# Prompt chunks of both mixers: two products from float32 to three float32r products of high and low parts

## What is computed

```python
# mLSTM, for each chunk of tokens (q, k: per head 128 wide; v: 256 wide)
A   = einsum('blhd,bshd->bhls', qc, kc) * exp(D - m_t)
num = einsum('bhls,bshv->bhlv', A, vc) + w_inter * einsum('blhd,bhdv->bhlv', qc, C)
den = sum(A) + w_inter * einsum('blhd,bhd->bhl', qc, n)
C   = decay * C + einsum('bshd,bshv->bhdv', kw, vc)
n   = decay * n + sum(kw)
# GLA, for each chunk
o = einsum('blhd,bhdv->blhv', qc * exp(Bc), S) + einsum('bhls,bshv->blhv', A, vc)
S = exp(BL) * S + einsum('bshd,bshv->bhdv', kc * exp(BL - Bc), vc)
```

## Time and profile before

| | |
|---|---|
| median of three runs | 2538.54 us |
| the profiled execution | 2539.21 us |
| its span | 2537.4 us |
| TensorE busy (16901 matmul records) | 2517.5 us, 99% |
| VectorE busy | 1675.8 us, 66% |
| ScalarE busy | 1072.3 us, 42% |
| mean granted TensorE clock | 0.999 |

### The profile page before, as it was taken

The page is one execution under the profiler, slowest core; times in us unless marked ns, Lnnn a source line. Parts: engine busy times, 40 slices in busy tenths (PEclk is TensorE's granted clock), DMA queues, the critical chain, the costliest instruction groups (busy, mean ns, idle before and its releaser), DMA issues.

```text
span 2537.4 us, 40969 instructions
## 1 busy us (share of the span) xinstructions
PE 2517.5 (99%) x16901; PEld 2276.0 (90%) x16901; DVE 1675.8 (66%) x2654; ACT 1072.3 (42%) x1568; POOL 0.2 (0%) x4
## 2 busy tenths in 40 slices
PE   9999999999999999999999999999999999999998
PEld 7899898887888999889998998998887988999998
DVE  6744575556457673357764778677876478888886
ACT  5343445442334442454533344446543344433333
POOL 0000000000000000000000000000000000000000
PEclk9999999999999999999999999999999999999999
DMA  6455544535433433453323343344436433333332
GB/s 227 138 173 162 148 150 141 156 110 178 146 102 119 137 96 100 154 170 109 96 84 125 117 135 119 123 155 141 122 106 191 145 129 117 88 100 100 96 100 100
DMA packets 176709, 330.41 MB, mean 130 GB/s; under 512 B 19964, under 2 KB 93436, under 8 KB 176524
## 3 DMA queue, kind: packets, MB, share of 16 engines
q1 hardware_dynamic: 176524, 327.79, 41.2%
HBM read 271.46 MB, written 56.28 MB: 129 GB/s over the span
## 4 chain that ended last, share of the span: by engine, by line
PE 91%; DVE 5%; ACT 2%; issue 1%; DMA 0%; SPq 0%; ACTq 0%; DVEq 0%
PE ps L1192 68%; PE ps L1320 10%; PE ps L1206 3%; PE ps L1570 1%; DVE Y L2438 1%; PE ps L1224 1%; PE ps L1512 1%; PE ps L1656 1%; DVE w_lo L2165 1%; PE ps L1501 1%; PE ps L1495 1%; ACT w_hi L1692 1%; PE ps L1374 1%; PE ps L1494 0%; PE ps L1603 0%
## 5 line engine op out<-in xcount | busy, mean ns | idle before, releaser
L1192 PE MATMUL ps<-HH,w_lo 128*128 128x288 f32 (+1 forms) x2680 | 902.4, 337 | 0.2 <-DVE w_lo L2165 0.2
L1192 PE MATMUL ps<-HL,w_hi 128*128 128x288 f32 (+1 forms) x2680 | 892.2, 333 | 0.0
L1192 PE MATMUL ps<-HH,w_hi 128*128 128x288 f32 (+1 forms) x2680 | 891.8, 333 | 0.0
L2165 DVE TENSOR_TENSOR w_lo<-w_stage,w_hi 128x1024 fp32r<-128x1024 f32 x392 | 478.4, 1221 | 178.3 <-ACT w_hi L1692 177.2
L1192 PEld LDWEIGHTS ps<-HH,w_lo 128*128 128x128 f32 x2680 | 502.9, 188 | 48.8 <-issue 5.8
L1192 PEld LDWEIGHTS ps<-HL,w_hi 128*128 128x128 f32 x2680 | 502.8, 188 | 42.7
L1192 PEld LDWEIGHTS ps<-HH,w_hi 128*128 128x128 f32 x2680 | 503.0, 188 | 41.6
L1692 ACT ACTIVATE w_hi<-w_stage 128x1024 fp32r<-128x1024 f32 x392 | 412.1, 1052 | 295.8 <-PE ps L1192 257.2
L1192 PE MATMUL ps<-hid_hi,w_lo 128*128 128x288 f32 (+1 forms) x1052 | 346.8, 330 | 1.9 <-DVE Y L2438 1.1
L1192 PE MATMUL ps<-hid_lo,w_hi 128*128 128x288 f32 (+1 forms) x1052 | 343.8, 327 | 0.0
L1192 PE MATMUL ps<-hid_hi,w_hi 128*128 128x288 f32 (+1 forms) x1052 | 343.6, 327 | 0.0
(11 more groups left out here) (336 smaller groups left out, 3271.5 us busy)
## 6 DMA issues: line engine op xcount, KB each, us to landing
w_stage<-w_gate_in SPq DMA_DIRECT2D x88, 512.0 KB, 3.7
w_stage<-w_up_in SPq DMA_DIRECT2D x88, 512.0 KB, 3.7
w_stage<-w_down_in SPq DMA_DIRECT2D x88, 512.0 KB, 3.7
w_stage<-w_in_in SPq DMA_DIRECT2D x80, 512.0 KB, 4.1
w_stage<-w_out_in SPq DMA_DIRECT2D x32, 512.0 KB, 3.8
proj_scratch<-evicted SPq DMA_DIRECT2D x48, 288.0 KB, 2.3
proj_scratch<-evicted SPq DMA_DIRECT2D x32, 256.0 KB, 2.1
w_stage<-w_v_in SPq DMA_DIRECT2D x16, 512.0 KB, 4.3
```

Of the source, the lines that this page charges most:

```text
L1192: mm = pe.matmul(ps[:, grp.bank + t, 0:W], wsl(w, k), x[:, k, t * W:(t + 1) * W], start=(k == first and m == 0), stop=(k == last and m == 2))
L2165: dve.tensor_tensor(g.wlo[:, n % NW, :], g.wst[:, n % NW, :], g.whi[:, n % NW, :].bitcast(F32), ALU.subtract).then_inc(s["w_lo"], 1)
```

## The change

For prompt chunks (0 to 7) in both mixers, keys (KW), values (V) and scores (A) are split: ScalarE copies each to float32r (KH, VH, AH), VectorE subtracts that from the original (KL, VL, AL). The two products become three float32r products each, summed in PSUM: low by high, high by low, high by high (`three`). The high values of mLSTM have two columns of ones. The product of queries and state stays float32 and comes after the three. KH, AH, VH and AL lie over buffers that are free at that time.

Where the splits stand: `k_high` at the end of "ma" (mLSTM) and in "l1" (GLA); `v_high` behind the copy of V in "mv" (chunks 4 to 7), in the new step "mp" (chunks 0 to 3) and in "l1"; `a_high` in "mp" and at the head of ScalarE's "lb"; `kv_low` and `a_low` on VectorE in "mp", and in GLA at the head of "l2" and of "lb". "mp" is tagged on unit a + 1, ahead of "mb" there: in block 0 that is b itself. TensorE's "mb" and "lb" wait for all three subtractions (kva_lo).

```diff
@@ mlstm
         if blk:
             tag(a + blk, "mv", c)
+        tag(a + 1, "mp", c)
         tag(b, "mb", c)
@@ TensorE
+            def three(out, high, low, vh, vl, stop=True):
+                pe.matmul(out, low, vh, start=True, stop=False)
+                pe.matmul(out[:, 0:DV], high, vl, start=False, stop=False)
+                return pe.matmul(out, high, vh, start=False, stop=stop)
             def mb(c):
                 pe.wait_ge(s["zeroed"], 1 + BLOCK(c))
-                pe.wait_ge(s["k_copied"], c + 1)
-                if c < 4:
-                    pe.wait_ge(s["values_landed"], 16 * (c + 1))
-                else:
-                    pe.wait_ge(s["v_copied"], TURNS(0, c))
                 pe.wait_ge(s["q_ready"], c + 1)
-                pe.wait_ge(s["scores"], c + 1)
+                pe.wait_ge(s["kva_lo"], 3 * c + 3)
                 for h in range(H):
+                    mm = three(ps[:, M0 + h, 0:DV + 2], g.AH[:, h, :], g.AL[:, h, :], g.VH[:, h, :], g.m.VL[:, h, 0:DV],
+                               c == 0)
                     if c:
-                        pe.matmul(ps[:, M0 + h, 0:DV + 1], g.m.QW[:, h, :], g.C[:, h, :], start=True, stop=False)
-                    mm = pe.matmul(ps[:, M0 + h, 0:DV + 1], g.m.A[:, h, :], g.m.V[:, h, :], start=c == 0, stop=True)
+                        mm = pe.matmul(ps[:, M0 + h, 0:DV + 1], g.m.QW[:, h, :], g.C[:, h, :], start=False, stop=True)
             def md(c):
-                    mm = pe.matmul(ps[:, M0 + h, 0:DV + 1], g.m.KW[:, h, :], g.m.V[:, h, :], start=True, stop=True)
+                    mm = three(ps[:, M0 + h, 0:DV + 2], g.KH[:, h, :], g.m.KL[:, h, :], g.VH[:, h, :], g.m.VL[:, h, 0:DV])
...
@@ ScalarE
+            def k_high(c, layer):
+                act.wait_ge(s["k_copied"], (NC + 1) * layer + c + 1)
+                wait(act, s["kv"], NC * layer + c)
+                act.activation(g.KH[:, :, :], (g.x if layer else g.m).KW[:, :, :], ACT.Copy).then_inc(s["kva_hi"], 1)
...
+            def a_high(c, layer):
+                if layer:
+                    act.wait_ge(s["merged"], 8 * c + 8)
+                else:
+                    act.wait_ge(s["scores"], c + 1)
+                wait(act, s["num"], NC * layer + c)
+                act.activation(g.AH[:, :, :], (g.x if layer else g.m).A[:, :, :], ACT.Copy).then_inc(s["kva_hi"], 1)
+            def mp(c):
+                if c < 4:
+                    v_high(c, 0)
+                a_high(c, 0)
+            def l1(c):
+                if c < NC:
+                    k_high(c, 1)
+                    v_high(c, 1)
             def lb(c):
                 x = g.x
+                a_high(c, 1)
                 exps()
@@ VectorE
+            def kv_low(c, layer):
+                x, i = g.x if layer else g.m, 3 * (NC * layer + c)
+                dve.wait_ge(s["kva_hi"], i + 1)
+                dve.tensor_tensor(x.KL[:, :, :], x.KW[:, :, :], g.KH[:, :, :].bitcast(F32), ALU.subtract
+                                  ).then_inc(s["kva_lo"], 1)
+                dve.wait_ge(s["kva_hi"], i + 2)
+                dve.tensor_tensor(x.VL[:, :, 0:DV], x.V[:, :, 0:DV], g.VH[:, :, 0:DV].bitcast(F32), ALU.subtract
+                                  ).then_inc(s["kva_lo"], 1)
+            def a_low(c, layer):
+                x = g.x if layer else g.m
+                dve.wait_ge(s["kva_hi"], 3 * (NC * layer + c) + 3)
+                dve.tensor_tensor(g.AL[:, :, :], x.A[:, :, :], g.AH[:, :, :].bitcast(F32), ALU.subtract
+                                  ).then_inc(s["kva_lo"], 1)
+            def mp(c):
+                kv_low(c, 0)
+                a_low(c, 0)
             def l2(c):
+                if c < NC:
+                    kv_low(c, 1)
                 merge(c, 4, NLV + 1)
             def lb(c):
                 x = g.x
+                a_low(c, 1)
```

More of the change, by code:

```diff
@@ L549, in memory @@
     g.S1L = nc.alloc_sbuf_tensor_at("s1_lo", [P, 512], F32R, offset=s1)
+    g.VH = nc.alloc_sbuf_tensor_at("v_hi", [P, H, DV + 2], F32R, offset=s1 - 3 * 2048)
+    g.KH = nc.alloc_sbuf_tensor_at("k_hi", [P, H, P], F32R, offset=t_end)
+    g.AH = nc.alloc_sbuf_tensor_at("scores_hi", [P, H, L], F32R, offset=t_end + 2048)
     g.Y = [sb(f"Y{b}", [P, KD, NT[b]]) for b in range(2)]
@@ L556, in memory @@
     g.E = sb("evicted", [P, 3, NT[1]])
+    up = nc.sbuf_base
     g.UP = sb("proj_sums", [P, 2, GW[1]])
+    g.AL = nc.alloc_sbuf_tensor_at("scores_lo", [P, H, L], F32R, offset=up)
     g.C = sb("state", [P, H, DV + 1])
@@ L608, in memory @@
     m = g.m = Program()
+    v = at["m"]
     m.V = piece("m", "v_one", [P, H, DV + 1])
+    m.VL = piece("m", "v_lo", [P, H, DV + 1], v, F32R)
+    k = at["m"]
     m.KW = piece("m", "k_weighted", [P, H, P])
+    m.KL = piece("m", "k_lo", [P, H, P], k, F32R)
     m.QW = piece("m", "q_weighted", [P, H, L])
@@ L628, in memory @@
     x.TT = piece("l", "y_gated", [P, KD, L], vt)
+    v = at["l"]
     x.V = piece("l", "v", [P, H, DV])
+    x.VL = piece("l", "v_lo", [P, H, DV], v, F32R)
+    k = at["l"]
     x.KW = piece("l", "k", [P, H, P])
+    x.KL = piece("l", "k_lo", [P, H, P], k, F32R)
     x.QW = piece("l", "q_decayed", [P, H, L])
@@ L668 @@
     "half_small", "outs", "y_stored",
-    "sums", "s_hi", "s_lo", "t_sum", "t_hi", "t_lo", "prod", "silu", "gated", "p_silu",
+    "sums", "s_hi", "s_lo", "t_sum", "t_hi", "t_lo", "prod", "silu", "gated", "p_silu", "kva_hi", "kva_lo",
 )
@@ L1595, in lb @@
                 x = g.x
-                if c < 4:
-                    pe.wait_ge(s["values_landed"], 16 * (4 + c + 1))
-                pe.wait_ge(s["merged"], 8 * c + 8)
                 pe.wait_ge(s["q_ready"], NC + 1 + c + 1)
+                pe.wait_ge(s["kva_lo"], 3 * (NC + c) + 3)
                 for h in range(H):
                     out = ps[:, M0 + h // 2, (h % 2) * DV:(h % 2 + 1) * DV]
+                    mm = three(out, g.AH[:, h, :], g.AL[:, h, :], g.VH[:, h, 0:DV], x.VL[:, h, :], c == 0)
                     if c:
-                        pe.matmul(out, x.QW[:, h, :], g.C[:, h, 0:DV], start=True, stop=False)
-                    mm = pe.matmul(out, x.A[:, h, :], x.V[:, h, :], start=c == 0, stop=True)
+                        mm = pe.matmul(out, x.QW[:, h, :], g.C[:, h, 0:DV], start=False, stop=True)
                 mm.then_inc(s["num"], 1)
                 for h in range(H):
-                    mm = pe.matmul(ps[:, M0 + 2 + h // 2, (h % 2) * DV:(h % 2 + 1) * DV], x.KW[:, h, :], x.V[:, h, :],
-                                   start=True, stop=True)
+                    mm = three(ps[:, M0 + 2 + h // 2, (h % 2) * DV:(h % 2 + 1) * DV], g.KH[:, h, :], x.KL[:, h, :],
+                               g.VH[:, h, 0:DV], x.VL[:, h, :])
                 mm.then_inc(s["kv"], 1)
@@ L1990, in ma, with v_high @@
                 ins.then_inc(s["k_copied"], 1)
+                if c < NC:
+                    k_high(c, 0)
+            def k_high(c, layer):
+                act.wait_ge(s["k_copied"], (NC + 1) * layer + c + 1)
+                wait(act, s["kv"], NC * layer + c)
+                act.activation(g.KH[:, :, :], (g.x if layer else g.m).KW[:, :, :], ACT.Copy).then_inc(s["kva_hi"], 1)
+            def v_high(c, layer):
+                if c < 4:
+                    act.wait_ge(s["values_landed"], 16 * (4 * layer + c + 1))
+                else:
+                    act.wait_ge(s["v_copied"], TURNS(layer, c))
+                wait(act, s["kv"], NC * layer + c)
+                act.activation(g.VH[:, :, 0:DV], (g.x if layer else g.m).V[:, :, 0:DV], ACT.Copy).then_inc(s["kva_hi"], 1)
+            def a_high(c, layer):
+                if layer:
+                    act.wait_ge(s["merged"], 8 * c + 8)
+                else:
+                    act.wait_ge(s["scores"], c + 1)
+                wait(act, s["num"], NC * layer + c)
+                act.activation(g.AH[:, :, :], (g.x if layer else g.m).A[:, :, :], ACT.Copy).then_inc(s["kva_hi"], 1)
+            def mp(c):
+                if c < 4:
+                    v_high(c, 0)
[4 more added lines that the diff above has]
+                    v_high(c, 1)
             def mv(c):
                 v_copy(c, 0, g.m.V)
+                if c < NC:
+                    v_high(c, 0)
             def v_copy(c, layer, V):
@@ L2121, in _ @@
                      "ma": ma, "mv": mv, "mb": mb, "me": me, "lg": lgate, "la0": la0, "la1": la1, "la2": la2, "la": la,
-                     "lb": lb, "le": le, "sh": sh}
+                     "lb": lb, "le": le, "sh": sh, "mp": mp, "l1": l1}
             hi(0)
@@ L2626, in ma @@
                 m = g.m
+                if c == 0:
+                    dve.tensor_copy(g.VH[:, :, DV:DV + 2], g.ones[:, 0:2 * H].rearrange("p (h o) -> p h o", o=2))
                 if c in (0, 4):
```

2 lines of the change are left out of this document (1 added, 1 removed).

## The result

The changed kernel takes **2631.65 us** (median of 4 runs, 2630.52 to 2633.16), the kernel before 2539.14 in the runs beside it (2538.36 to 2540.22): a ratio of 1.0363, 95% interval 1.0351 to 1.0375. It is 92.5 us slower; forecast were 2612 and a range of 2590 to 2631, so the median lies just outside (two of the four runs, 2630.52 and 2630.60, lie inside).

What follows compares the result with a forecast made beforehand. TensorE, busy 99% of the span, was taken to bound the kernel. Profiled 2539.2 + 70.9 waits + 12 clock - 9.2 saving = 2612.9, median 0.7 lower: 2612 us, range 2590 to 2631.

Steps and rivals of the forecast that it cites:

- What bounds the kernel: TensorE, busy 99% of the span, sets the end time; work added to VectorE or ScalarE costs only where TensorE waits.
- The cost of the products: On TensorE, three float32r products at 0.120 us replace one float32 at 0.433 us, saving 9.2 us over 128 products.
- The waits: TensorE waits for late splits in 15 of 16 chunks of mLSTM and GLA, 70.9 us in all.
- The clock: TensorE's clock halves behind the six GLA waits of about 7 us, costing 12 us.
- Below 5 us I assume none: TensorE waits shorter than 5 us, here 2.2 to 4.3 us, bring no fall of the clock and cost nothing there.
- the clock falls in the shorter waits too: Rival: nine more TensorE waits also halve the clock, at 2.0 us each, giving 2630 us; chance 0.13.
- The price of a fall: Coming back to whole clock on TensorE costs 2.0 us per fall, half of the 4.0 us at the trace's start.
- The range: For the whole kernel, 2590 to 2631 us, taking in the clock's rivals and leaving out the last ones.

Runs made afterwards that it cites:

- experiment 2: Kernel of experiment 1 with one float32 product in place of each three float32r ones, splits and waits as there: 2552.52 us.
- experiment 4: Changed kernel with the split of the GLA scores put ahead of the next chunk's gating, on the same unit: 2602.58 us, ratio 1.0247.
- experiment 1: Changed kernel with splits one unit ahead of their product (mLSTM product one unit later, GLA scores' split one unit earlier): 2542.97 us, ratio 1.0014.
- experiment 3: Changed kernel with useless float32 matmuls on TensorE filling nearly the length of each new wait: 2601.65 us, ratio 1.0246.
- experiment 5: Kernel before with 36 waits for VectorE additions set into TensorE's dense matmuls, meant to last about 1 to 6 us: 2765.97 us, ratio 1.0893.
- 6: Kernel before with only mLSTM's product step "mb" moved one unit later: 2546.04 us, ratio 1.0028.
- 7: Changed kernel with only keys by values in three products, scores by values left float32 and unsplit: 2536.42 us, ratio 0.9988.

## Why the prediction was right, and where it was wrong

**What bounds the kernel** held: TensorE's time is the kernel's time. Everything that TensorE lost or won shows in the span, one for one, in after and in all seven experiments within 3 us.

**The cost of the products** held. The line between 288 and 512 columns gave 0.120 us, the trace of after has 0.12; 9.2 us were forecast, experiment 2 has 9.0 to 9.9. The Trainium skill's formula for isolated matmuls ("TensorE: Matmul & The Clock Gate", section "Back-to-back issue gap") gives 109 ns and 13.6 us in all; these products, each with its weight load, start 117 to 120 ns apart, so the measurement is against using it here.

**The waits** held, in number, place and size:

| place | forecast | measured |
|---|---|---|
| mLSTM chunk 0 | 3.3 | 3.6 |
| chunks 1 to 3 | 4.3, 4.2, 4.2 | 4.6, 4.6, 4.6 |
| chunk 4 | 0 | 0 |
| chunks 5 to 7 | 2.15 each | 2.6, 2.5, 2.5 |
| GLA 0 to 2, 4 to 6 | 7.14, 6.95 | 7.3, 7.2 |
| GLA 3, 7 | 3.1, 2.9 | 3.3, 3.3 |
| all | 70.9 | 70.2 idle |

The measured ones of a place are from the start of the matmul ahead to the start of the product, which are 0.13 to 0.23 us apart where nothing is waited for; the last row is idle time. Measured as the forecast counted, from the old start to the new one, they sum to 72.5 us, 1.6 more than forecast. Reading the queues instead of busy shares was enough for this: ScalarE has 58% of its time free, and TensorE still waits 7 us for it. That the exponentials are the cause in GLA, experiment 4 shows; that the places are the cause of the waits, experiment 1.

**The clock** is the step that failed: "Below 5 us I assume none". The mechanism was in the sum, but for six waits of 15, at 2.0 us each: 12 us. Measured are 16 falls, which cost 27.9 us by experiment 3 (31.0 by half of the busy time). The six long waits took 11.9 of it, just what was forecast; the ten falls that were put at nothing, behind nine new waits of 2.1 to 4.3 us and an old one of 2.0, took 16.0. With the 1.6 us of longer waits that is the whole miss of the profiled execution, 2630.6 against 2612.9. The assumption came from two rows: one wait of 2.1 us without a fall, and one fall that was seen 5.1 us after the last matmul. The first shows what may happen at 2.1 us, not what does: the same wait, 2.0 us long, had a fall behind it in after, and in experiment 5 five of six idle stretches of 2.1 to 2.3 us had one. The second was read as if the 5 us were needed; it bounds from above only. Between 2.1 and 5 us the trace of before has nothing, and nine waits lay there. The forecast put all nine on the side of the upper row. The rival "the clock falls in the shorter waits too" took the other side, with 2630 us, and is what happened; it had a chance of 0.13. The Trainium skill ("TensorE: Matmul & The Clock Gate", section "Part 1: The HAM clock gate") spoke for it, with its rule that idle gaps between bursts put TensorE back to half clock and that the moment of a change varies. The traces here agree on both: 16 falls in after, and a wait of 3.05 us with a fall and one without in experiment 4. But the page warns of longer gaps than the four of 2.0 to 2.2 us behind which the clock fell in after, so that by the page alone these would have stood at nothing.

**The price of a fall**, 2.0 us, was right for the six long waits (11.9 us in experiment 3's count) and somewhat high for the others (16.0 in ten, 1.6 each). It came from a single recovery, at the start of the trace (half of 4.0 us), and single falls cost 1.2 to 2.8: that the six come out at 2.0 so closely is in part luck.

**The range** ended at 2631, at 2630 and the rounding; the median is 0.65 above. The rival had counted 15 falls at 2.0, which is 2 us more than all 16 cost. The 16th, behind a wait that the change didn't touch, was in no step.

What stays open: why the fall comes behind one wait and not behind its equal, at 2 us (experiment 5) and even at 3 (experiment 4). The runs show that it does, not what decides.

## What to carry to other kernels

Price a new wait of the engine that sets the end twice, once for its length and once for the clock: here nearly every wait from 2.1 us up cost 1.2 to 2.8 us more than it lasted, so three short ones are dearer than a long one of the same sum. When inputs of a product get a further step (a split, a cast, a copy), look where that step is queued, not how long it takes: 88.7 of the 92.5 us went away by moving steps. And look for the part of the change whose inputs have cover already; here the keys alone gave 2 to 3 us, the whole change took 92.

## What was not expected of the hardware

- A useless matmul can be cheaper than an idle engine: 161 of them, some 70 us, made the kernel 30.0 us faster, since the stretches that they filled would else have been idle.
- In experiment 5 the clock was never halved behind idle stretches up to 2.05 us (11 of them), behind five of six from 2.09 to 2.34 us, and behind all 24 from 3.26 us on. Length alone doesn't decide it there: one and the same wait, for proj_sums, had no fall behind it in the kernel before (2.12 us) and in experiments 3, 5, 6 and 7 (1.97 to 2.05), and had one in after (2.00) and in experiments 1, 2 and 4 (1.88 to 1.96). In experiment 4 two waits of 2.86 and 3.05 us had none.
- A fall costs little more behind a long wait than behind a short one. By half of the busy time it is 2.3 us on average behind the six waits of 7 us in after and 1.7 behind the other ten; in experiment 5, where the waits went up to 11.6 us, it is 1.5 to 3.1. The same wait of 3.2 us (mLSTM chunk 0) cost 1.4 us in after and 2.8 in experiment 4.
- At half clock a float32r product of 256 columns is 0.21 us from start to start, at whole clock 0.12: 1.8 times, not twice. That is why half of the busy time at half clock (31.0 us) is more than the clock cost (27.9).
